# Attention logits of rows 0-127 and the indexer's dot products as three products of rounded parts, in a two-layer encoder on one core

## The chip, the core and the metric

The kernel runs on one NeuronCore of a Trainium2 chip as one launch. The metric is device time in microseconds (us). Five engines run in parallel, each through its own instructions in order: TensorE (PE, matmuls and transposes, its weight loads shown apart as PEld), VectorE (DVE), ScalarE (ACT), GpSimd (POOL) and SyncE (SP, which issues DMAs). They meet only at semaphores.

## The reference, cut to what matters

Two layers over 256 tokens of width 1024. All data is 32-bit float. In each layer:

```
h = rmsnorm(x);  z = h @ w_in          # split into qa ka va qi ki wi ga qb kb vb gb
# group A: 8 heads of 64, sparse attention
dots   = qi . ki / 8                   # 4 index heads of 64
iscore = sum_h relu(dots) * wi         # top 64 admissible keys of each query are kept
oa     = softmax(qa . ka / 8 over the kept keys) @ va
# group B: 4 heads of two maps, differential attention
ob = rmsnorm((softmax(q1 k1) - lambda softmax(q2 k2)) @ vb)
y  = concat(oa * silu(ga), ob * silu(gb)) @ w_out;  x = x + rmsnorm(y)
x  = x + rmsnorm((p @ w_ple_proj) * sigmoid(x @ w_ple_gate))
```

Rows 0 to 127 see keys 0 to 127 only; rows 128 to 255 see all 256. The change touches `dots` and the logits `qa . ka` and `q . k` of rows 0 to 127. The numbers computed stay the same but for rounding.

## The kernel before

**Tiling.** The tokens are two row blocks, b = 0 and b = 1, of 128 rows. Weights stream in as units of 256 rows by 512 columns (256 by 324 for the indexer's chunk). A large product is made of rounded parts: ScalarE copies a unit into a rounded 32-bit type (`w_hi`), VectorE subtracts that from the original (`w_lo`), and a matmul becomes three: high by high, low by high, high by low. One unit by one row block is a "piece": two groups of these three matmuls, 128 by 512. The activations are split in the same way (`act_hi`, `act_lo`).

**Order.** The function `layer_steps` writes one list of steps for a layer, and every engine walks the same list and does its part of each step. Pieces are the backbone; the attention steps are hung between them by the table `PLACE`, whose numbers count pieces from the first piece of the KB chunk (`mid`). Steps in the same slot are ordered by `rank`. `all_steps` adds the splitting of the next weight units (`HIGH` on ScalarE, `LOW` on VectorE).

**The steps the change touches.**
- `T chunk b`: PE transposes the four 128 by 128 tiles of a projected chunk into the one PSUM bank `tr` (L1332), and others empty it. For K, both blocks, and for Q, b = 1, ScalarE copies it rounded into `k_hi` or `q_hi` and VectorE then writes `k_lo` or `q_lo` (L934, L930). For Q, b = 0, ScalarE alone copies it whole into `qT`; for K, b = 0, ScalarE first makes a whole copy `kT` too.
- `TI b`: the same for the indexer's three tiles (L1321), copied whole by ScalarE into `idxT`, which lies in the memory of `pT`.
- `D`: the dot products (L1343), whole 32-bit matmuls, 64 rows deep. Odd and even heads use the two halves of the array's rows. ScalarE applies relu, VectorE sums the scores (L946, L948).
- `S n`: the logits (L1166). For b = 1 three products of `q_hi`, `q_lo`, `k_hi`, `k_lo`, 256 columns; for b = 0 one whole matmul `qT` by `kT`, 128 columns.
- `topk b r`: one round of the selection on VectorE (L961, L962); eight rounds for each block.
- `PT n`: PE transposes mixed probabilities into `tr` (L1375).

**One bank, one counter.** `TI`, `T` and `PT` all use `tr`. Each may start only when the previous user's bank is emptied: `wait_tr` waits on the counter `tr_out`, which the last reader of a step raises. In the trace a whole 32-bit matmul shows as two records, a rounded one as one.

Of the kernel before, what the change touches and what calls it, by code (L numbers as in the profile page):

```python
# [58 lines left out]
for _i, _u in enumerate(UNITS):  # L59
# [21 lines left out]
    S=[12, 15, 18, 34, 42, 43],  # L81
# [13 lines left out]
def layer_steps(L):  # L95
# [45 lines left out]
    else:  # L141
# [5 lines left out]
        mms("QB", one(1), {2: [("TI", 1)], 3: [("D",)]})  # L147

    mid = [[] for _ in range(7 * len(both))]
    placed = [(PLACE["lam"], ("lam",)), (PLACE["glu"], ("glu", 0))]  # L150
# [66 lines left out]
def build(nc, x, p, pre_norm_g, w_in, w_out, post_norm_g, lambda_q1, lambda_k1, lambda_q2, lambda_k2, subln_g,  # L217
# [6 lines left out]
    with ctx:  # L224
        def sb(name, shape, dt=fp32):
            return ctx.enter_context(nc.sbuf_tensor(name, shape, dt))
# [25 lines left out]
        k_lo = sb("k_lo", [P, 4, SEQ], f32r)  # L252
        q_hi = sb("q_hi", [P, 4, P], f32r)
        q_lo = sb("q_lo", [P, 4, P], f32r)

# [4 lines left out]
        idxT = pT[:, 0:2, :, :].rearrange("p a t q -> p (a t q)")[:, 0:3 * SEQ].rearrange("p (j t) -> p j t", j=3)  # L260
# [61 lines left out]
        qk_hi_done = sem("qk_hi_done")  # L322
        dots_done, relu_done, score_done = sem("dots_done"), sem("relu_done"), sem("score_done")
# [58 lines left out]
        QK_WHOLE = [("QB", 0), ("QA", 0)]  # L382
        QK_SPLIT = [s[1:] for s in tr_steps if s[0] == "T" and s[1:] not in QK_WHOLE]

# [209 lines left out]
        def _(act):  # L594
# [29 lines left out]
            for pos, (L, s) in enumerate(STEPS):  # L624
# [78 lines left out]
                elif kind == "TI":  # L703
                    b = s[1]
                    act.wait_ge(tr_done, tr_index(L, s))
                    copy(idxT[:, :, b * P:(b + 1) * P], tr[:, 0:3 * P].rearrange("p (j t) -> p j t", j=3))\
                        .then_inc(tr_out, 1)
                elif kind == "T":
                    chunk, b = s[1:]
                    act.wait_ge(tr_done, tr_index(L, s))  # L710
                    g, src = int(chunk[1] == "A"), tr[:, :].rearrange("p (j t) -> p j t", j=4)

                    if chunk[0] == "Q" and b == 0:
                        copy(qT[g][:, :, 0:P], src, HEAD ** -0.5).then_inc(tr_out, 1)
                    elif chunk[0] == "Q":
                        copy(q_hi[:, :, :], src, HEAD ** -0.5).then_inc(qk_hi_done, 1)
                    else:
                        if b == 0:
                            copy(kT[:, :, :], src)
                        copy(k_hi[:, :, b * P:(b + 1) * P], src).then_inc(qk_hi_done, 1)  # L720
# [76 lines left out]
        def _(dve):  # L797
# [31 lines left out]
            for pos, (L, s) in enumerate(STEPS):  # L829
# [94 lines left out]
                elif kind == "T" and s[1:] not in QK_WHOLE:  # L924
# [3 lines left out]
                    dve.wait_ge(qk_hi_done, L * 6 + QK_SPLIT.index(s[1:]) + 1)  # L928
                    if chunk[0] == "Q":
                        ins = nc.vector.scalar_tensor_tensor(q_lo[:, :, :], src, HEAD ** -0.5,  # L930
                                                             q_hi[:, :, :].bitcast(fp32), ALU.mult,
                                                             ALU.subtract)
# [3 lines left out]
                    ins.then_inc(tr_out, 1)  # L936
                elif kind == "D":
# [154 lines left out]
        def _(pe):  # L1092
# [60 lines left out]
            def logits(L, n, g, b, keys):  # L1153

                for j in range(N // keys):
                    for part in range(1 if b == 0 else 3):
                        for odd in range(2):
                            m = s_task(2 * n + odd)[2][j]
                            rows = slice(odd * HEAD, (odd + 1) * HEAD)
                            if b == 0:  # L1160
                                q, k = qT[g][rows, m // 2, 0:P], kT[rows, m // 2, :]
                            else:
                                q = (q_lo if part == 2 else q_hi)[rows, m // 2, :]
                                k = (k_lo if part == 1 else k_hi)[rows, m // 2, :]
                            end = part == (0 if b == 0 else 2)
# [20 lines left out]
            for pos, (L, s) in enumerate(STEPS):  # L1186
# [147 lines left out]
                elif kind == "D":  # L1334
# [3 lines left out]
                    for b in range(NB):  # L1338
                        keys = (b + 1) * P
                        for j in range(2):  # L1340
                            for odd in range(2):
                                rows = slice(odd * HEAD, (odd + 1) * HEAD)
                                ins = nc.tensor.matmul(dots_of(b, odd)[:, j * keys:(j + 1) * keys],  # L1343
                                                       idxT[rows, j, b * P:(b + 1) * P], idxT[rows, 2, 0:keys],
                                                       start=True, stop=True)
                                if j == 1:
                                    ins.then_inc(dots_done, 1)
# [82 lines left out]
```

## Time and profile before

| | us |
|---|---|
| median of 3 runs (lowest, highest) | 359.07 (358.68, 359.42) |
| the profiled execution's own time | 359.26 |
| its span, first to last instruction | 357.5 |
| PE busy | 350.0 (98%) |
| PE weight loads busy | 291.9 (82%) |
| VectorE busy | 264.5 (74%) |
| ScalarE busy | 228.6 (64%) |
| GpSimd busy | 67.2 (19%) |

The granted TensorE clock was 0.997 of full speed over the span. Busy time of PE overlaps its own pipeline (the next matmul starts before the last one's modelled end), so what a step of PE costs is read from the distance of two starts, not from the length of one record. The profiled execution is 1.76 us longer than its span and 0.19 us above the median of the runs.

### The profile page before, as it was taken

The page shows a single profiled execution, that of the slowest core. Times are in us where ns is not written, and L with a number is a line of the kernel's source. Part 1 is how long each engine was busy: PE and PEld are TensorE (multiplying, and loading weights), DVE is VectorE, ACT ScalarE, POOL GpSimd, SP SyncE. Part 2 cuts the span into 40 slices and gives each one's busy share as a digit, 9 for nine tenths or more (in the row PEclk, how much of TensorE's full clock was granted, in tenths as well). Part 3 has the DMA queues.
Part 4 walks back from the last instruction along what each step waited for, and adds up shares of the span by engine and source line. Part 5 has one row for each costly group of instructions (what it writes and reads, how often), then busy time and mean ns, then how long its engine had stood idle before and what let it go on. Part 6 is the DMA issues. An engine that isn't in the chain of part 4 may idle for free.

```text
span 357.5 us, 5709 instructions
## 1 busy us (share of the span) xinstructions
PE 350.0 (98%) x1927; PEld 291.9 (82%) x1927; DVE 264.5 (74%) x562; ACT 228.6 (64%) x459; POOL 67.2 (19%) x121
## 2 busy tenths in 40 slices
PE   8999999999999999999999999999999999999992
PEld 7887888888888888888888888788888888888882
DVE  3886979988946766786797487988895668678543
ACT  4897557777678945555757665778658686365221
POOL 1076261142200000013106433014220000000000
PEclk9999999999999999999999999999999999999998
DMA  7996488762754454647575927556355446550011
GB/s 287 381 336 216 130 193 200 257 177 68 224 169 131 129 195 149 210 158 154 179 231 158 353 82 207 147 129 178 107 168 155 151 141 213 175 169 11 0 50 69
DMA packets 31820, 61.12 MB, mean 171 GB/s; under 512 B 2376, under 2 KB 4432, under 8 KB 31792
## 3 DMA queue, kind: packets, MB, share of 16 engines
q1 hardware_dynamic: 30656, 57.48, 50.5%
q0 software_dynamic: 1120, 3.28, 4.8%
q8 instruction: 16, 0.26, 0.3%
q14 instruction: 12, 0.10, 0.1%
q10 hardware_dynamic: 16, 0.00, 0.0%
HBM read 59.71 MB, written 1.05 MB: 170 GB/s over the span
## 4 chain that ended last, share of the span: by engine, by line
PE 96%; issue 2%; DVE 1%; ACT 0%; POOLq 0%; DVEq 0%; POOL 0%
PE proj L1233 26%; PE proj L1235 25%; PE proj L1234 25%; PE sc L1314 3%; PE tr L1375 2%; PE sc L1166 2%; PE tr L1332 2%; PE pv L1396 2%; PE pv L1391 1%; PE proj L1177 1%; PE proj L1150 1%; PE proj L1166 1%; PE proj L1246 1%; PE proj L1139 1%; PE sc L1184 1%
## 5 line engine op out<-in xcount | busy, mean ns | idle before, releaser
L1233 PE MATMUL proj<-w_hi,act_hi 128*128 128x512 f32 (+1 forms) x392 | 157.4, 402 | 0.0
L1235 PE MATMUL proj<-w_hi,act_lo 128*128 128x512 f32 (+1 forms) x392 | 152.2, 388 | 0.0
L1234 PE MATMUL proj<-w_lo,act_hi 128*128 128x512 f32 (+1 forms) x392 | 151.6, 387 | 0.0
L835 DVE TENSOR_TENSOR w_lo<-raw,w_hi 128x1024 fp32r<-128x1024 f32 (+1 forms) x102 | 121.6, 1210 | 11.1 <-ACT w_hi L596 10.5
L596 ACT ACTIVATE w_hi<-raw 128x1024 fp32r<-128x1024 f32 (+2 forms) x103 | 102.5, 1022 | 2.4 <-PE proj L1235 1.8
L1235 PEld LDWEIGHTS proj<-w_hi,act_lo 128*128 128x128 f32 x392 | 73.5, 188 | 15.5
L1233 PEld LDWEIGHTS proj<-w_hi,act_hi 128*128 128x128 f32 x392 | 73.7, 188 | 14.6 <-issue 1.0
L1234 PEld LDWEIGHTS proj<-w_lo,act_hi 128*128 128x128 f32 x392 | 73.8, 188 | 12.8
L537 POOL TENSOR_TENSOR rstd<-var,minus_half 128x1 f32<-128x1 f32 x12 | 7.6, 640 | 191.6 <-DVE var L823 162.7
L732 ACT ACTIVATE probs<-probs,neg_max 128x128 f32<-128x128 f32 (+1 forms) x64 | 28.2, 444 | 6.0 <-DVE neg_max L986 6.0
L527 POOL TENSOR_TENSOR v_all<-work,rot_tab 128x128 f32<-128x128 f32 x16 | 10.6, 664 | 77.6 <-ACT work L596 77.5
L596 ACT ACTIVATE act_hi<-sc 128x512 fp32r<-128x512 f32 x20 | 11.3, 598 | 17.6 <-PE sc L1314 16.0
L596 ACT ACTIVATE pT<-tr 128x512 f32<-128x512 f32 (+1 forms) x20 | 11.4, 572 | 10.2 <-PE tr L1375 6.9
L915 DVE TENSOR_TENSOR act_lo<-sc,act_hi 128x512 fp32r<-128x512 f32 x16 | 10.4, 684 | 5.9 <-ACT act_hi L596 5.9
L934 DVE TENSOR_TENSOR k_lo<-tr,k_hi 128x512 fp32r<-128x512 f32 x8 | 5.5, 688 | 10.5 <-ACT k_hi L596 10.5
L732 ACT ACTIVATION_READ_ACCUMULATOR probs<-probs,neg_max 128x1 f32 x64 | 12.1, 189 | 0.0
L961 DVE MAX8 top<-score 128x8 f32<-128x128 f32 (+1 forms) x32 | 11.5, 358 | 0.6
L1375 PEld LDWEIGHTS tr<-ident,probs 128*128 128x128 f32 x72 | 8.8, 140 | 2.7 <-ACT pT L596 0.7
L962 DVE MATCH_REPLACE8 score<-top,score 128x128 f32<-128x128 f32 (+1 forms) x32 | 11.0, 343 | 0.0
L1375 PE MATMUL tr<-ident,probs 128*128 128x128 f32 x72 | 10.9, 273 | 0.0
L1051 DVE TENSOR_TENSOR work<-work,emb 128x512 f32<-128x512 f32 x7 | 4.8, 687 | 7.2 <-ACT work L768 7.2
L528 POOL TENSOR_TENSOR v_all<-work,rot_tab 128x64 f32<-128x64 f32 x16 | 10.1, 632 | 0.0
(209 smaller groups left out, 441.1 us busy)
## 6 DMA issues: line engine op xcount, KB each, us to landing
raw<-in_w_in_dram SPq DMA_DIRECT2D x59, 512.0 KB, 4.2
raw<-in_w_out_dram SPq DMA_DIRECT2D x16, 512.0 KB, 3.4
raw<-in_w_ple_gate_dram SPq DMA_DIRECT2D x16, 512.0 KB, 3.7
raw<-in_w_in_dram SPq DMA_DIRECT2D x7, 324.0 KB, 5.0
raw<-in_w_ple_proj_dram SPq DMA_DIRECT2D x4, 512.0 KB, 4.2
resid<-in_x_dram SPq DMA_DIRECT2D x2, 512.0 KB, 6.2
probs<-in_w_in_dram SPq DMA_DIRECT2D x2, 512.0 KB, 9.2
g_ple<-in_ple_norm_g_dram POOLq DMA_DIRECT2D x2, 512.0 KB, 7.3
```

The costliest lines, as they stand in the source:

```text
L527: nc.gpsimd.tensor_tensor(rot_a[:, 0:heads, :], view[:, :, 0:ROT], table(cos2, slice(0, ROT)), ALU.mult)
L596: return nc.scalar.activation(dst, src, ACT.Copy, scale=scale)
L732: last = nc.scalar.activation(probs[:, i % 4, j * keys:(j + 1) * keys], probs[:, i % 4, j * keys:(j + 1) * keys], ACT.Exp, bias=neg_max[:, ...
L835: nc.vector.tensor_tensor(w_lo[:, g % SLOTS, 0:nk * cols], landing(g, nk * cols), w_hi[:, g % SLOTS, 0:nk * cols].bitcast(fp32), ALU.subtr ...
L961: link(nc.vector.max(top8[:, :], score[b][:, :]))
L962: link(nc.vector.match_replace(score[b][:, :], top8[:, :], score[b][:, :], TAKEN))
L1166: ins = nc.tensor.matmul(s_bank(2 * n + odd)[:, j * keys:(j + 1) * keys], q, k, start=(part == 0), stop=end)
L1233: nc.tensor.matmul(ps, src_hi[:, b, k0 + k, :], hi, start=(first_u and k == 0), stop=False)
L1234: nc.tensor.matmul(ps, src_hi[:, b, k0 + k, :], lo, start=False, stop=False)
L1235: last = nc.tensor.matmul(ps, src_lo[:, b, k0 + k, :], hi, start=False, stop=last_k)
L1314: last = nc.tensor.transpose(sc[i % 2][:, j * P:(j + 1) * P], tile, ident[:, :])
L1375: last = nc.tensor.transpose(tr[:, j * P:(j + 1) * P], probs[:, si % 4, col:col + P], ident[:, :])
```

## The change

- The dot products of the indexer are made of rounded parts. ScalarE copies `tr` into `idx_hi`, VectorE writes `idx_lo` (both lie in `k_hi` and `k_lo`, which are free then), and VectorE, not ScalarE, now raises `tr_out`. Each of the 8 whole matmuls of a layer becomes three.
- The logits of rows 0 to 127 are made of rounded parts too. ScalarE writes `q0_hi`, VectorE `q0_lo` (in the memory of `p_hi` and `p_lo`) and raises `tr_out`. The whole copies `qT` and `kT` go. The 8 whole matmuls of each of the two groups become 24. Step `S` now waits for `k_lo`, not for `k_hi`.
- In layer 1 step `D` stands after the first piece of KB, not after the last of QB. In both layers step `S 3` (group A, rows 0 to 127) stands at slot 35, not 34.

```diff
-    S=[12, 15, 18, 34, 42, 43],
+    S=[12, 15, 18, 35, 42, 43],
...
-        mms("QB", one(1), {2: [("TI", 1)], 3: [("D",)]})
+        mms("QB", one(1), {2: [("TI", 1)]})
 
     mid = [[] for _ in range(7 * len(both))]
+    if L > 0:
+        mid[0].append(("D",))
...
+        idx_hi, idx_lo = k_hi[:, 0:3, :], k_lo[:, 0:3, :]
...
+        q0_hi, q0_lo = (tile[:, :, :, :].rearrange("p b k t -> p (b k) t") for tile in (p_hi, p_lo))
...
-        QK_WHOLE = [("QB", 0), ("QA", 0)]
-        QK_SPLIT = [s[1:] for s in tr_steps if s[0] == "T" and s[1:] not in QK_WHOLE]
+        QK_SPLIT = [s[1:] for s in tr_steps if s[0] == "T"]
...
                 elif kind == "TI":
                     b = s[1]
                     act.wait_ge(tr_done, tr_index(L, s))
-                    copy(idxT[:, :, b * P:(b + 1) * P], tr[:, 0:3 * P].rearrange("p (j t) -> p j t", j=3))\
-                        .then_inc(tr_out, 1)
+                    copy(idx_hi[:, :, b * P:(b + 1) * P], tr[:, 0:3 * P].rearrange("p (j t) -> p j t", j=3))\
+                        .then_inc(idx_hi_done, 1)
...
-                    if chunk[0] == "Q" and b == 0:
-                        copy(qT[g][:, :, 0:P], src, HEAD ** -0.5).then_inc(tr_out, 1)
-                    elif chunk[0] == "Q":
-                        copy(q_hi[:, :, :], src, HEAD ** -0.5).then_inc(qk_hi_done, 1)
+                    if chunk[0] == "Q":
+                        copy((q_hi if b else q0_hi)[:, :, :], src, HEAD ** -0.5).then_inc(qk_hi_done, 1)
                     else:
-                        if b == 0:
-                            copy(kT[:, :, :], src)
                         copy(k_hi[:, :, b * P:(b + 1) * P], src).then_inc(qk_hi_done, 1)
...
-                elif kind == "T" and s[1:] not in QK_WHOLE:
+                elif kind == "T":
...
-                    dve.wait_ge(qk_hi_done, L * 6 + QK_SPLIT.index(s[1:]) + 1)
+                    dve.wait_ge(qk_hi_done, L * 8 + QK_SPLIT.index(s[1:]) + 1)
                     if chunk[0] == "Q":
-                        ins = nc.vector.scalar_tensor_tensor(q_lo[:, :, :], src, HEAD ** -0.5,
-                                                             q_hi[:, :, :].bitcast(fp32), ALU.mult,
-                                                             ALU.subtract)
+                        hi, lo = (q_hi, q_lo) if b else (q0_hi, q0_lo)
+                        ins = nc.vector.scalar_tensor_tensor(lo[:, :, :], src, HEAD ** -0.5,
+                                                             hi[:, :, :].bitcast(fp32), ALU.mult, ALU.subtract)
...
+                elif kind == "TI":
+                    b = s[1]
+                    cols = slice(b * P, (b + 1) * P)
+                    dve.wait_ge(idx_hi_done, L * 2 + b + 1)
+                    nc.vector.tensor_tensor(idx_lo[:, :, cols], tr[:, 0:3 * P].rearrange("p (j t) -> p j t", j=3),
+                                            idx_hi[:, :, cols].bitcast(fp32), ALU.subtract).then_inc(tr_out, 1)
...
                 for j in range(N // keys):
-                    for part in range(1 if b == 0 else 3):
+                    for part in range(3):
                         for odd in range(2):
...
-                            if b == 0:
-                                q, k = qT[g][rows, m // 2, 0:P], kT[rows, m // 2, :]
-                            else:
-                                q = (q_lo if part == 2 else q_hi)[rows, m // 2, :]
-                                k = (k_lo if part == 1 else k_hi)[rows, m // 2, :]
-                            end = part == (0 if b == 0 else 2)
+                            hi, lo = (q_hi, q_lo) if b else (q0_hi, q0_lo)
+                            q = (lo if part == 2 else hi)[rows, m // 2, :]
+                            k = (k_lo if part == 1 else k_hi)[rows, m // 2, 0:keys]
+                            end = part == 2
...
                         for j in range(2):
-                            for odd in range(2):
+                            for part, odd in [(part, odd) for part in range(3) for odd in range(2)]:
...
+                                q, k = idx_lo if part == 2 else idx_hi, idx_lo if part == 1 else idx_hi
...
-                    if b == 0:
-                        pe.wait_ge(qk_hi_done, L * 6 + QK_SPLIT.index(keys_from) + 1)
-                    else:
-                        pe.wait_ge(tr_out, tr_index(L, ("T",) + keys_from))
+                    pe.wait_ge(tr_out, tr_index(L, ("T",) + keys_from))
```

How the instructions move, in the order in which each engine has them.

VectorE in layer 0, group A: the rounds of the selection for rows 128 to 255 (MAX, MATCH_REPLACE on `score`) around `T QA 0`. Before:

```order
L1010 SCALAR_TENSOR_TENSOR probs<-probs,mix_c 128x256
L961 MAX top<-score 128x8
L962 MATCH_REPLACE score<-top,score 128x256 [waits dve_chain]
L961 MAX top<-score 128x8 [waits dve_chain]
L962 MATCH_REPLACE score<-top,score 128x256 [waits dve_chain]
L961 MAX top<-score 128x8 [waits dve_chain]
L962 MATCH_REPLACE score<-top,score 128x256 [waits dve_chain]
L835 TENSOR_TENSOR w_lo<-raw,w_hi 128x1024 [waits hi_done,dve_chain]
```

After (`p_lo<-tr,p_hi` is `q0_lo`):

```order
L1016 SCALAR_TENSOR_TENSOR probs<-probs,mix_c 128x256
L967 MAX top<-score 128x8
L968 MATCH_REPLACE score<-top,score 128x256 [waits dve_chain]
L967 MAX top<-score 128x8 [waits dve_chain]
L968 MATCH_REPLACE score<-top,score 128x256 [waits dve_chain]
L931 SCALAR_TENSOR_TENSOR p_lo<-tr,p_hi 128x512 [waits qk_hi_done,dve_chain]
L967 MAX top<-score 128x8
L968 MATCH_REPLACE score<-top,score 128x256 [waits dve_chain]
L835 TENSOR_TENSOR w_lo<-raw,w_hi 128x1024 [waits hi_done,dve_chain]
```

A subtraction now stands behind the second of three rounds in a row; nothing stood there before. Layer 1 has the same rows at its own `T QA 0`.

PE in layer 1, the end of the QB chunk; `tr` and `pv` are the banks of the dot products. Before:

```order
L1235 MATMUL proj<-w_hi,act_lo 128x512
L1343 MATMUL tr<-pT 128x128 [waits at_lo,tr_out]
L1343 MATMUL pv<-pT 128x128
L1343 MATMUL tr<-pT 128x128
L1343 MATMUL pv<-pT 128x128
L1343 MATMUL sc<-pT 128x256 x4
L1233 MATMUL proj<-w_hi,act_hi 128x512 [waits at_lo,lo_done,idx_out]
L1234 MATMUL proj<-w_lo,act_hi 128x512
L1235 MATMUL proj<-w_hi,act_lo 128x512
L1233 MATMUL proj<-w_hi,act_hi 128x512
L1234 MATMUL proj<-w_lo,act_hi 128x512
L1235 MATMUL proj<-w_hi,act_lo 128x512
```

After (`k_hi` and `k_lo` hold `idx_hi` and `idx_lo`):

```order
L1237 MATMUL proj<-w_hi,act_hi 128x512 [waits at_lo,lo_done,idx_out]
L1238 MATMUL proj<-w_lo,act_hi 128x512
L1239 MATMUL proj<-w_hi,act_lo 128x512
L1237 MATMUL proj<-w_hi,act_hi 128x512
L1238 MATMUL proj<-w_lo,act_hi 128x512
L1239 MATMUL proj<-w_hi,act_lo 128x512
L1348 MATMUL tr<-k_hi 128x128 [waits at_lo,tr_out]
L1348 MATMUL pv<-k_hi 128x128
L1348 MATMUL tr<-k_lo,k_hi 128x128
L1348 MATMUL pv<-k_lo,k_hi 128x128
L1348 MATMUL tr<-k_hi,k_lo 128x128
L1348 MATMUL pv<-k_hi,k_lo 128x128
```

The dot products stand one piece, six matmuls, later, and are now single products of parts.

PE in layer 0, the logits of rows 0 to 127 of group B. Before:

```order
L1332 MATMUL tr<-ident,work 128x128 [waits rope_z,tr_out]
L1332 MATMUL tr<-ident,work 128x128 x3
L1166 MATMUL sc<-kT,qT_b 128x128 [waits relu_done,qk_hi_done]
L1166 MATMUL sc<-kT,qT_b 128x128 x7
L1233 MATMUL proj<-w_hi,act_hi 128x512 [waits at_lo,lo_done]
L1234 MATMUL proj<-w_lo,act_hi 128x512
L1235 MATMUL proj<-w_hi,act_lo 128x512
```

After (`p_hi` and `p_lo` hold `q0_hi` and `q0_lo`):

```order
L1336 MATMUL tr<-ident,work 128x128 [waits rope_z,tr_out]
L1336 MATMUL tr<-ident,work 128x128 x3
L1170 MATMUL sc<-k_hi,p_hi 128x128 [waits relu_done,tr_out]
L1170 MATMUL sc<-k_hi,p_hi 128x128
L1170 MATMUL sc<-k_lo,p_hi 128x128 x2
L1170 MATMUL sc<-k_hi,p_lo 128x128 x2
L1170 MATMUL sc<-k_hi,p_hi 128x128 x2
L1170 MATMUL sc<-k_lo,p_hi 128x128 x2
```

Eight matmuls became 24 (the pattern goes on for all four pairs of maps), and the wait is for `tr_out` in place of `qk_hi_done`.

## Rows read from the trace of the kernel before

**Rows 1.** Page: busy time, slices of VectorE, granted clock, chain by engine, w_lo.

```profile
PE 350.0 (98%) x1927; PEld 291.9 (82%) x1927; DVE 264.5 (74%) x562; ACT 228.6 (64%) x459; POOL 67.2 (19%) x121
...
DVE  3886979988946766786797487988895668678543
...
PEclk9999999999999999999999999999999999999998
...
PE 96%; issue 2%; DVE 1%; ACT 0%; POOLq 0%; DVEq 0%; POOL 0%
...
L835 DVE TENSOR_TENSOR w_lo<-raw,w_hi 128x1024 fp32r<-128x1024 f32 (+1 forms) x102 | 121.6, 1210 | 11.1 <-ACT w_hi L596 10.5
```

**Rows 2.** Timeline, PE, layer 0: start us, length us, engine, line, operation, count.

```profile
33.13 0.37 PE L1343 MATMUL tr<-pT 64*128 64x128 f32 x1
33.35 0.27 PE L1343 MATMUL tr<-pT 64*128 64x128 f32 x1
33.46 0.27 PE L1343 MATMUL tr<-pT 64*128 64x128 f32 x1
33.68 1.03 PE L1343 MATMUL sc<-pT 64*128 64x256 f32 x8
34.65 0.50 PE L1233 MATMUL proj<-w_hi,act_hi 128*128 128x512 f32 x1
```

**Rows 3.** Timeline, PE, layer 0: logits of rows 0-127, both head groups.

```profile
54.46 1.16 PE L1166 MATMUL sc<-kT,qT_b 64*128 64x128 f32 x16
...
93.13 1.16 PE L1166 MATMUL sc<-kT,qT_a 64*128 64x128 f32 x16
```

**Rows 4.** Timeline, PE, layer 0: logits of rows 128-255, second and last step.

```profile
60.10 0.28 PE L1166 MATMUL sc<-k_lo,q_hi 64*128 64x256 f32 x2
...
61.28 0.28 PE L1166 MATMUL proj<-k_hi,q_lo 64*128 64x256 f32 x2
```

**Rows 5.** Timeline, weight loads at the same place, the first two.

```profile
59.87 0.19 PEld L1166 LDWEIGHTS sc<-k_hi,q_hi 64*128 64x128 f32 x2 [0.35 <-issue]
59.98 0.19 PEld L1166 LDWEIGHTS sc<-k_lo,q_hi 64*128 64x128 f32 x2
```

**Rows 6.** Timeline, PE, layer 0: query transposes of group A, then probabilities.

```profile
77.99 0.60 PE L1332 MATMUL tr<-ident,work 128*128 128x128 f32 x4
...
79.36 0.39 PE L1234 MATMUL proj<-w_lo,act_hi 128*128 128x512 f32 x1
79.58 0.39 PE L1235 MATMUL proj<-w_hi,act_lo 128*128 128x512 f32 x1
79.81 0.60 PE L1375 MATMUL tr<-ident,probs 128*128 128x128 f32 x4
```

**Rows 7.** Timeline, ScalarE and VectorE, same stretch.

```profile
78.62 0.60 ACT L596 ACTIVATE qT_a<-tr 128x512 f32<-128x512 f32 x1 [0.46 <-PE tr L1332]
...
80.15 0.41 DVE L962 MATCH_REPLACE8 score<-top,score 128x256 f32<-128x256 f32 x1
80.59 0.43 DVE L961 MAX8 top<-score 128x8 f32<-128x256 f32 x1
```

**Rows 8.** Timeline, PE and VectorE, layer 1, the same place.

```profile
251.84 0.60 PE L1375 MATMUL tr<-ident,probs 128*128 128x128 f32 x4
...
252.54 0.43 DVE L961 MAX8 top<-score 128x8 f32<-128x256 f32 x1
```

**Rows 9.** Timeline, layer 1: the low part of group B, and who waits.

```profile
214.68 0.69 DVE L930 SCALAR_TENSOR_TENSOR q_lo<-tr,q_hi 128x512 fp32r<-128x512 f32 x1
...
215.42 0.42 PEld L1332 LDWEIGHTS tr<-ident,work 128*128 128x128 f32 x4 [0.33 <-DVE q_lo L930]
```

**Rows 10.** Timeline, layer 1: second index transposes copied, scores start.

```profile
203.78 0.49 ACT L596 ACTIVATE pT<-tr 128x384 f32<-128x384 f32 x1 [2.51 <-PE tr L1321]
...
206.51 0.43 DVE L946 TENSOR_SCALAR score<-probs,w_idx 128x128 f32<-128x128 f32 x1 [3.78 <-ACT probs L725]
```

**Rows 11.** Timeline, VectorE, layer 0: the low part of group A keys.

```profile
93.23 0.68 DVE L934 TENSOR_TENSOR k_lo<-tr,k_hi 128x512 fp32r<-128x512 f32 x1
```

More of the change, by code:

```diff
@@ L259, in build @@
         pT = sb("pT", [P, 3, 4, P])
-        idxT = pT[:, 0:2, :, :].rearrange("p a t q -> p (a t q)")[:, 0:3 * SEQ].rearrange("p (j t) -> p j t", j=3)
         score = [sb("score0", [P, P]), sb("score1", [P, SEQ])]
@@ L322, in build @@
         qk_hi_done = sem("qk_hi_done")
+        idx_hi_done = sem("idx_hi_done")
         dots_done, relu_done, score_done = sem("dots_done"), sem("relu_done"), sem("score_done")
@@ L710, in _ @@
                     act.wait_ge(tr_done, tr_index(L, s))
-                    g, src = int(chunk[1] == "A"), tr[:, :].rearrange("p (j t) -> p j t", j=4)
-                    if chunk[0] == "Q" and b == 0:
-                        copy(qT[g][:, :, 0:P], src, HEAD ** -0.5).then_inc(tr_out, 1)
-                    elif chunk[0] == "Q":
-                        copy(q_hi[:, :, :], src, HEAD ** -0.5).then_inc(qk_hi_done, 1)
-                    else:
-                        if b == 0:
-                            copy(kT[:, :, :], src)
+                    src = tr[:, :].rearrange("p (j t) -> p j t", j=4)
+                    if chunk[0] == "Q":
+                        copy((q_hi if b else q0_hi)[:, :, :], src, HEAD ** -0.5).then_inc(qk_hi_done, 1)
+                    else:
                         copy(k_hi[:, :, b * P:(b + 1) * P], src).then_inc(qk_hi_done, 1)
@@ L1340, in _ @@
                         for j in range(2):
-                            for odd in range(2):
+                            for part, odd in [(part, odd) for part in range(3) for odd in range(2)]:
                                 rows = slice(odd * HEAD, (odd + 1) * HEAD)
+                                q, k = idx_lo if part == 2 else idx_hi, idx_lo if part == 1 else idx_hi
                                 ins = nc.tensor.matmul(dots_of(b, odd)[:, j * keys:(j + 1) * keys],
-                                                       idxT[rows, j, b * P:(b + 1) * P], idxT[rows, 2, 0:keys],
-                                                       start=True, stop=True)
-                                if j == 1:
+                                                       q[rows, j, b * P:(b + 1) * P], k[rows, 2, 0:keys],
+                                                       start=(part == 0), stop=(part == 2))
+                                if j == 1 and part == 2:
                                     ins.then_inc(dots_done, 1)
```

## The prediction

> **What bounds the kernel.** First the page: PE is busy 98% of the span, at a granted clock of 0.9 or more in all slices but the last, and the chain that ended last runs over PE for 96% of its length [rows 1]. So what is added to PE's own work is added to the time, nearly one for one, and so is every stretch in which PE waits. VectorE is busy 74%, but not evenly: in many slices it stands at 8 or 9 tenths [rows 1]. That it has 93 us free over the span says nothing on a place where its queue is full. So I then read the timeline of PE at the steps that the change rewrites [rows 2 to 4], the weight loads there [rows 5], and the queues of VectorE and ScalarE at each step whose release of `tr` goes over to VectorE [rows 6 to 11].
>
> **What a step of PE costs.** Odd and even heads run as pairs on the two halves of the array; a pair is one step. Whole 32-bit at 128 columns: two records for each matmul, and the starts stand 0.11 us apart (33.35, 33.46) [rows 2]; 0.1115 with the next digit taken from whole blocks: 16 records of a block of logits take 1.16 us, of which 0.27 is the last one's own length and 0.10 the first load, and 0.78 over seven steps is 0.112 [rows 2, 3]. Whole at 256 columns: 8 records, 1.03 less a last length of 0.38, 0.65 over three steps, 0.216 [rows 2]. Rounded at 256 columns: from 60.10 to 61.28 lie ten steps, 0.118 each [rows 4]. Rounded at 128 columns is in no row; this is the disputed price p.
>
> Bounds of p. Below: rounded at 256 columns costs 0.118 and at 512 columns 0.22 to 0.23 (79.36 to 79.58 and to 79.81) [rows 4, 6]; the line through these, 0.11 per 256 columns, gives 0.06 at 128. Above: a narrow rounded matmul could be no better than a whole one of its size, two steps of 0.1115, 0.223 [rows 2]. Between them: at the head of a block, where nothing streams yet and PE's loader had been idle for 0.35 us, the second rounded weight load starts 0.11 us after the first (59.87, 59.98) [rows 5]. At that point only the load itself can hold it back, so a load takes about 0.11 us, and as each step needs one, 128 columns can't go faster than that however fast they stream. I take p = 0.1115, as for the whole ones, which load 128 columns too.
>
> The Trainium skill (TensorE: Matmul & The Clock Gate, "Back-to-back issue gap") gives about 81 ns for a matmul with its load at 128 columns in a long stream. By it the PE terms below would come to +0.1 us and not +1.9. No run here shows a step of 81 ns; the loads 0.11 us apart speak against it [rows 5].
>
> **Sum on PE.** Logits of rows 0 to 127: four blocks (two groups, two layers) of 8 steps become four of 12. Dot products of rows 0 to 127: two blocks of 4 become two of 6. Together 40 steps of 0.1115 = 4.46 become 60 p = 6.69: +2.23. Dot products of rows 128 to 255: 8 whole steps of 0.216 = 1.73 become 12 rounded of 0.118 = 1.42: -0.31. PE: +1.9. The gaps at the ends of such a block (first load, change to the halved array and back) are there with both kinds and don't change.
>
> **The wait I expect.** `T QA 0` leaves its transposes in `tr` at 78.4 (77.99 + four of 0.11) [rows 6]. Now ScalarE copies them at 78.62 and, by 79.22, frees `tr` [rows 7]; PE has one piece to do and begins `PT 2` in the same bank at 79.81 without a wait [rows 6]. After the change `tr` is free only when VectorE has written `q0_lo`. In its queue that stands behind the second of three rounds of the selection, and that round ends at 80.56, the third begins at 80.59 [rows 7]. Those rounds are paced by what lies before them (softmax of `S 2`, which PE and ScalarE feed), so they don't come earlier. `q0_lo` has the form of `q_lo`, 0.69 us [rows 9], so it ends at 81.28, and PE's load follows 0.05 later, as 215.42 follows 215.37 in [rows 9]: 81.33 in place of 79.81, 1.52, and 0.06 for the load that is no longer ahead. 1.58 us. Behind `PT 2` everything of PE is queued, so the loss is whole. Layer 1: 252.54 + 0.74 = 253.28 against 251.84 [rows 8], 1.44 + 0.06 = 1.50. Sum +3.1. If VectorE should come to it earlier, the term is 0; that is the lower end.
>
> **Other steps that now end on VectorE.** `T QB 0`: four pieces lie before the next use of `tr`, over 5 us; hidden. `TI 0`, `TI 1`: ScalarE's copy ends at 204.27 and the subtraction of 384 columns is shorter than 0.69 [rows 9, 10], so `idx_lo` is there by 204.9 to 205.0. `D` stood at 205.07; one piece later, after 205.07 + 6 x 0.23 = 206.45, it has 1.4 us of room. In layer 0 `D` has two pieces behind `TI 1`; hidden. The kT copies that go (two for each layer, 0.60 each by the same form of copy [rows 7]) are off the chain: 0.
>
> The move of `D` has a price on VectorE. The scores of layer 1 begin at 206.51, after VectorE was idle 3.78 us [rows 10]; they now begin one piece, 1.38, and two steps of 0.11 later, 1.6. One `w_lo`, 1.21 [rows 1], goes from behind them into that idle time before them. Net, VectorE reaches `q_lo` of `T QB 1` some 0.4 later. PE already waits there, though briefly: its load starts at 215.42, after 0.33 us of idling, released by `q_lo` [rows 9]. PE itself comes 0.06 later, so +0.35. In layer 0 the same place gets its dot products 0.2 later, and I take +0.1 for it by likeness. Together +0.5, between 0 and 0.9.
>
> `S 3` waits for `k_lo`: it ends at 93.23 + 0.68 = 93.91 [rows 11]. `S 3` stood at 93.13 [rows 3] and would have waited 0.8; at its new slot it comes at 94.5, later still by the 1.6 above, and even with VectorE 0.7 later it has room: 0. The slot takes one piece, 1.4 us, from the time before `PT 3` (slot 40), which needs the softmax of `S 3` and the bank; five pieces, 6.9 us, are left between them, and I take them as enough: 0.
>
> **Sum.** 1.9 + 3.1 + 0.5 = 5.5. On the profiled execution, 359.26, that is 364.8; it stands 0.19 above the median, so the forecast for the median is 359.07 + 5.5 = 364.6.
>
> **Rivals.**
> A, the above: 364.6, own range 363 to 366.5.
> B, narrow rounded matmuls cost as much as whole ones of their size, p = 0.223. 60 p = 13.4, so PE gets +8.9 - 0.3 = +8.6, and with both waits 359.07 + 8.6 + 3.6 = 371.2. For it: no row shows a rounded matmul below 256 columns. Against it: nothing from 512 to 256 columns hints at a fixed price, and the loads give a reason for 0.11 only.
> C, narrow steps stream at the columns' rate, p = 0.06: 3.6 - 4.5 - 0.3 = -1.2, with both waits and 0.2 less of the small ones, 359.07 + 2.2 = 361.2. For it: the line from 512 to 256 columns. Against it: [rows 5]. The Trainium skill (same page, "Weight-path perf modes") says that fast weight load is on for 128 weights of a type that is not FP32; were the rounded type such a one, C would be the case. The loads 0.11 us apart in this trace don't show it.
> D, the wait at `PT 2` doesn't form and p is 0.1115: 359.07 + 1.9 + 0.5 = 361.5. It would need VectorE to come to `q0_lo` by 79.1, 1.5 us before the trace has it there.
> E, not slower: the subtraction is taken before the rounds, so no wait forms at `PT 2`, and what is left hangs on p alone: 60 p - 4.46 - 0.31 + 0.5 is 0 at p = 0.071. Below this the kernel gains, at 0.06 by 0.7 us: 358.4. Place: `PT 2` in both layers. Against it both [rows 5] and [rows 7].
>
> **How the numbers follow.** A 0.57, B 0.21, C 0.13, D 0.06, E 0.03. The predicted time is A's. The range goes from 361.1, which takes in C and D, to 371.6 with B; about 0.15 is left out. What a measurement of this kernel can tell from no change is some 0.2%, 0.7 us: all but E lie beyond it. E is shared between faster, 0.02, and within, 0.01, with 0.01 more for what I have not seen; slower 0.96.
>
> **What would show it.** In the profile after: PE's pairs at 128 columns 0.11 us apart (0.06: C; 0.22, or two records for each matmul: B). An idle time of PE's loader of some 1.5 us before the transposes of probabilities of `PT 2`, put down to VectorE's `p_lo`, twice; none there would be D. One of 0.7 before the second QB transposes of layer 1, put down to `q_lo`. The dot products of rows 128 to 255 at 0.118 a step. PE busy up by about 2 us, less than the span. I am wrong if the span grows by less than 3 us or by more than 8.

## The result and the profile after

| | before | after |
|---|---|---|
| median, us (4 runs each, side by side) | 359.25 | 363.73 |
| lowest, highest | 358.68, 359.53 | 363.49, 364.12 |
| span of the profiled execution | 357.5 | 361.8 |

The ratio is 1.0128, with a 95% interval from 1.0114 to 1.0142: 4.5 us slower (4.1 to 5.1).

The page of the kernel after: busy times, and the chain that ended last by engine.

```profile
PE 351.7 (97%) x1975; PEld 293.8 (81%) x1975; DVE 268.7 (74%) x570; ACT 226.8 (63%) x455; POOL 67.5 (19%) x121
...
PE 92%; DVE 3%; issue 2%; ACT 2%; POOLq 0%; DVEq 0%; POOL 0%
```

Against [rows 1], PE is busy only 1.7 us more, though the span grew by 4.3: less than half is matmul work. The share of VectorE in the chain went from 1% to 3%, that of ScalarE from 0% to 2%. So at some places PE is now released by VectorE, behind work that ScalarE feeds.

The timeline of PE at the logits of rows 0 to 127 of group B, layer 0, after (12 steps; the first three and the last, and what follows):

```profile
54.10 0.33 PE L1170 MATMUL sc<-k_hi,p_hi 64*128 64x128 f32 x2
54.26 0.28 PE L1170 MATMUL sc<-k_lo,p_hi 64*128 64x128 f32 x2
54.37 0.28 PE L1170 MATMUL sc<-k_hi,p_lo 64*128 64x128 f32 x2
...
55.38 0.28 PE L1170 MATMUL sc<-k_hi,p_lo 64*128 64x128 f32 x2
55.59 0.51 PE L1237 MATMUL proj<-w_hi,act_hi 128*128 128x512 f32 x1
```

From the second start, 54.26, to the twelfth, 55.38, lie ten steps: 0.112 us each, the price of a whole step of that width [rows 2, 3]. The first step takes 0.16 (54.10 to 54.26), where the first whole one took 0.22 (33.13 to 33.35 in [rows 2]). So the block should be longer by four steps, 0.45, less 0.05. The starts say the same: it and the way to the next piece took 1.49 us (54.10 to 55.59), where the block before took 1.09 (54.46 [rows 3] to 55.55).

The timeline of PE's weight loads at the next place, `PT 2` of layer 0, after (in brackets the idle time before, and who ended it), and then that of VectorE in the same stretch:

```profile
79.37 0.19 PEld L1239 LDWEIGHTS proj<-w_hi,act_lo 128*128 128x128 f32 x1
81.36 0.42 PEld L1377 LDWEIGHTS tr<-ident,probs 128*128 128x128 f32 x4 [1.81 <-DVE p_lo L931]
81.75 0.19 PEld L1237 LDWEIGHTS proj<-w_hi,act_hi 128*128 128x128 f32 x1
```

```profile
78.66 0.42 DVE L967 MAX8 top<-score 128x8 f32<-128x256 f32 x1
...
79.64 0.43 DVE L967 MAX8 top<-score 128x8 f32<-128x256 f32 x1
...
80.18 0.41 DVE L968 MATCH_REPLACE8 score<-top,score 128x256 f32<-128x256 f32 x1
80.62 0.69 DVE L931 SCALAR_TENSOR_TENSOR p_lo<-tr,p_hi 128x512 fp32r<-128x512 f32 x1
81.23 0.42 DVE L967 MAX8 top<-score 128x8 f32<-128x256 f32 x1
```

This answers to [rows 6, 7]. The probabilities' transposes began at 79.81, right behind the piece before them [rows 6]; now their weight load comes at 81.36, after 1.81 us in which the loader idled, released by `p_lo`, VectorE's subtraction for `q0_lo`. That begins at 80.62, behind two rounds of the selection (78.66 and 79.64, so 0.98 us a round), where the third stood (80.59 in [rows 7]). The chain that ended last, in order of time, runs here from ScalarE's exponentials over the mixing of the maps and these two rounds to the subtraction. Two of its pieces, the exponentials and the last one ahead of PE:

```profile
75.77 1.48 ACT probs L732 x6
...
80.62 0.70 DVE p_lo L931
```

The subtraction and the load that it releases in layer 1, from the same timelines:

```profile
255.02 0.69 DVE L931 SCALAR_TENSOR_TENSOR p_lo<-tr,p_hi 128x512 fp32r<-128x512 f32 x1
255.76 0.42 PEld L1377 LDWEIGHTS tr<-ident,probs 128*128 128x128 f32 x4 [1.72 <-DVE p_lo L931]
```

### The profile page after: what moved, and what is told of

Read it like the earlier page. It is cut to its first block, busy times and chain, and to the rows that moved or that the text cites. A ratio compares the mean times of both kernels' runs of the same rounds, so it can differ in the third digit from the quotient of the medians.

```text
span 361.8 us, 5811 instructions
## 1 busy us (share of the span) xinstructions
PE 351.7 (97%) x1975; PEld 293.8 (81%) x1975; DVE 268.7 (74%) x570; ACT 226.8 (63%) x455; POOL 67.5 (19%) x121
## 4 chain that ended last, share of the span: by engine, by line
PE 92%; DVE 3%; issue 2%; ACT 2%; POOLq 0%; DVEq 0%; POOL 0%
PE proj L1237 25%; PE proj L1239 24%; PE proj L1238 24%; PE sc L1170 3%; PE sc L1318 2%; PE tr L1377 2%; PE tr L1336 2%; PE pv L1398 2%; PE proj L1156 1%; PE proj L1181 1%; ACT probs L732 1%; PE pv L1393 1%; PE proj L1170 1%; PE proj L1145 1%; PE sc L1188 1%
## 5 line engine op out<-in xcount | busy, mean ns | idle before, releaser
L1237 PE MATMUL proj<-w_hi,act_hi 128*128 128x512 f32 (+1 forms) x392 | 157.5, 402 | 0.0
L1237 PEld LDWEIGHTS proj<-w_hi,act_hi 128*128 128x128 f32 x392 | 73.7, 188 | 14.0 <-issue 0.3
L600 ACT ACTIVATE pT<-tr 128x512 f32<-128x512 f32 x16 | 9.5, 595 | 9.7 <-PE tr L1377 9.7
L600 ACT ACTIVATE k_hi<-tr 128x512 fp32r<-128x512 f32 (+1 forms) x12 | 6.7, 559 | 11.4 <-PE tr L1336 7.8
L536 POOL TENSOR_TENSOR work<-v_all 128x128 f32<-128x128 f32 x16 | 10.3, 643 | 1.3
```

Source lines behind the costliest of these rows:

```text
L600: return nc.scalar.activation(dst, src, ACT.Copy, scale=scale)
L1237: nc.tensor.matmul(ps, src_hi[:, b, k0 + k, :], hi, start=(first_u and k == 0), stop=False)
```

## Where the time went, place by place

The start-up of an execution differs: the first whole piece of PE's steady work begins at 21.35 us in the profile before, at 20.84 in the one after, and between 20.99 and 23.99 in those of the experiments. So I took the start of the first matmul of each group of three, of which a piece has two (L1233 before, L1237 after, the same line of code, 400 of them), in each trace, and read where its distance from the same start before changes. Everything from 21 us on is in this table, in us; the columns are the kernels, the last row is the sum of all changes of the distance to the end of the span.

| place | after | wait_only | logits_only | dots_only | rounds0 | rounds1 | pt2_later | s34_pt27 | half_load |
|---|---|---|---|---|---|---|---|---|---|
| dot products and `q_lo`, layer 0 | +0.16 | 0 | 0 | +0.14 | +0.15 | +0.04 | +0.04 | +0.14 | +0.15 |
| logits group B, layer 0 | +0.36 | 0 | +0.36 | 0 | +0.36 | +0.36 | +0.35 | +0.36 | -0.26 |
| `PT 2`, layer 0 | +1.59 | +1.55 | +1.58 | 0 | +0.24 | +0.57 | +0.21 | +0.21 | +1.58 |
| logits group A, layer 0 | +0.41 | 0 | +0.41 | 0 | +0.41 | +0.41 | +0.41 | +1.22 | -0.23 |
| dot products and `q_lo`, layer 1 | +0.04 | 0 | 0 | +0.03 | +0.03 | +0.03 | +0.04 | +0.03 | +0.04 |
| logits group B, layer 1 | +0.39 | 0 | +0.39 | 0 | +0.39 | +0.39 | +0.39 | +0.39 | -0.23 |
| `PT 2`, layer 1 | +1.52 | +1.53 | +1.48 | 0 | +0.26 | +0.53 | +0.14 | +0.14 | +1.48 |
| logits group A, layer 1 | +0.41 | 0 | +0.41 | 0 | +0.41 | +0.41 | +0.41 | +1.17 | -0.23 |
| all from 21 us on | +4.88 | +2.89 | +4.57 | +0.02 | +2.20 | +2.70 | +2.00 | +3.61 | +2.30 |

Changes below 0.03 are written as 0. Two traces are not in the table, d_old and rounds1_pt27; their sums stand with their runs. A column's places add up to its last row within 0.2: some hundredths lie between the places, and that is how fine this comparison of two executions is. The profile after thus holds 3.1 us of waits at `PT 2`, 1.6 of logits, 0.2 at the dot products and `q_lo`, and it started 0.5 sooner: 4.9 - 0.5 = 4.4, against 4.3 in the spans.

## The experiments

Medians are of the runs of that kernel, with those of the kernel before on the same chip beside them.

| kernel | median | before beside it | ratio (95% interval) |
|---|---|---|---|
| wait_only | 362.28 | 359.23 | 1.0087 (1.0062 to 1.0113) |
| logits_only | 364.92 | 359.23 | 1.0149 (1.0122 to 1.0176) |
| dots_only | 359.51 | 359.23 | 1.0002 (0.9983 to 1.0020) |
| pt2_later | 361.03 | 359.23 | 1.0047 (1.0032 to 1.0061) |
| rounds0 | 362.64 | 359.38 | 1.0083 (1.0058 to 1.0108) |
| half_load | 361.71 | 359.38 | 1.0063 (1.0040 to 1.0086) |
| s34_pt27 | 362.97 | 359.38 | 1.0102 (1.0075 to 1.0130) |
| d_old | 364.52 | 359.38 | 1.0145 (1.0120 to 1.0170) |
| rounds1 | 362.25 | 359.04 | 1.0089 (1.0076 to 1.0102) |
| rounds1_pt27 | 361.10 | 359.04 | 1.0071 (1.0051 to 1.0092) |

An interval is up to 2 us wide, and the medians hold the start-up, which moves by more than the differences in question. So differences of some tenths are read from the table of places and not from the medians.

**The wait alone** (on the kernel before).

```diff
...
-                    if chunk[0] == "Q" and b == 0:
+                    if chunk == "QA" and b == 0:
+                        copy(qT[g][:, :, 0:P], src, HEAD ** -0.5).then_inc(qa0_done, 1)
+                    elif chunk[0] == "Q" and b == 0:
...
+                elif kind == "T" and s[1:] == ("QA", 0):
+                    dve.wait_ge(qa0_done, L + 1)
+                    nc.vector.scalar_tensor_tensor(p_lo[:, :, :, :].rearrange("p b k t -> p (b k) t"),
+                                                   tr[:, :].rearrange("p (j t) -> p j t", j=4), HEAD ** -0.5,
+                                                   qT[1][:, :, 0:P], ALU.mult, ALU.subtract).then_inc(tr_out, 1)
```

> The kernel before, with one thing added: at T QA 0, in both layers, VectorE subtracts from tr (its result, written to the free low part of p, is used by nobody), and VectorE in place of ScalarE raises tr_out. No matmul changes. Theory A (the late release of tr makes PE wait at PT 2, and the wait is paid in full): 3.1 us slower than before, 362.3; loader idle of 1.8 before PT 2 in each layer, put down to that VectorE instruction. Rival (the wait is made up by other engines' slack, and the time of the change is matmul work): within 0.5 us of before.

3.05 us slower by the medians, 2.9 by the trace from 21 us on. The timeline of the weight loads and of VectorE in its trace, at `PT 2` of layer 0:

```profile
80.89 0.19 PEld L1243 LDWEIGHTS proj<-w_hi,act_lo 128*128 128x128 f32 x1
...
82.12 0.69 DVE L929 SCALAR_TENSOR_TENSOR p_lo<-tr,qT_a 128x512 fp32r<-128x512 f32 x1
82.86 0.20 PEld L1383 LDWEIGHTS tr<-ident,probs 128*128 128x128 f32 x2 [1.79 <-DVE p_lo L929]
```

Not one matmul is changed here, and the wait is the same, 1.79 us of an idle loader. Theory A holds: one late release of `tr` in each layer costs PE 1.5 to 1.6 us, and at most 0.2 of the 3.1 us is given back later.

**The logits alone** (on the kernel after).

```diff
-        mms("QB", one(1), {2: [("TI", 1)]})
+        mms("QB", one(1), {2: [("TI", 1)], 3: [("D",)]})
...
-    if L > 0:
-        mid[0].append(("D",))
...
-                    copy(idx_hi[:, :, b * P:(b + 1) * P], tr[:, 0:3 * P].rearrange("p (j t) -> p j t", j=3))\
-                        .then_inc(idx_hi_done, 1)
+                    copy(idxT[:, :, b * P:(b + 1) * P], tr[:, 0:3 * P].rearrange("p (j t) -> p j t", j=3))\
+                        .then_inc(tr_out, 1)
...
-                            for part, odd in [(part, odd) for part in range(3) for odd in range(2)]:
+                            for odd in range(2):
```

> The changed kernel with the index heads' part undone: dot products whole again, D at its old place in layer 1. The logits of rows 0 to 127 stay in three products. Theory A: 1.55 us of matmuls (four blocks, 0.39 each as measured after) and 3.1 us of waits: 4.6 slower than before, 363.8 or 0.3 less than after. If the index part costs more than its matmuls show, 362.5 or less.

By the places 4.6 us from 21 us on, as expected. The median says 5.7, 1.1 more than expected; the six runs spread from 363.55 to 365.93, and the interval, 4.4 to 6.3, takes in the 4.6. The places say 0.3 less than after, which is what the index part adds there.

**The dot products alone** (on the kernel before; `D` of layer 1 one piece later, as in the change).

```diff
-        mms("QB", one(1), {2: [("TI", 1)], 3: [("D",)]})
+        mms("QB", one(1), {2: [("TI", 1)]})
...
+    if L > 0:
+        mid[0].append(("D",))
...
-                    copy(idxT[:, :, b * P:(b + 1) * P], tr[:, 0:3 * P].rearrange("p (j t) -> p j t", j=3))\
-                        .then_inc(tr_out, 1)
+                    copy(idx_hi[:, :, b * P:(b + 1) * P], tr[:, 0:3 * P].rearrange("p (j t) -> p j t", j=3))\
+                        .then_inc(idx_hi_done, 1)
...
+                elif kind == "TI":
...
-                            for odd in range(2):
+                            for part, odd in [(part, odd) for part in range(3) for odd in range(2)]:
```

> The kernel before with the index heads' part of the change alone: dot products from rounded parts in three products, D of layer 1 one piece later. Theory A: matmuls +0.07 in each layer, +0.1 for q_lo in layer 0, nothing in layer 1: 0.3 us slower than before, 359.5, hardly to be told from it. Rival (VectorE's two more subtractions in each layer push the chain of selection and so PE): 1 us or more slower.

Not to be told from the kernel before: 1.0002, and 0.7 us slower at the upper end of the interval. The places show 0.14 in layer 0 and 0.03 in layer 1, and the rest of its sum is below what such a comparison of two executions resolves. The rival, that two more subtractions for each layer push VectorE's chain and cost 1 us or more, is out.

**`PT 2` one slot later** (on the kernel after).

```diff
-    PT=[19, 23, 26, 40, 41, 45, 46, 50, 51],
+    PT=[19, 23, 27, 40, 41, 45, 46, 50, 51],
```

> The changed kernel with PT 2 one slot later (27 in place of 26), one more piece between the transposes of T QA 0 and the next use of tr. Theory A: q0_lo ends at 81.3, PE comes at 81.2, so the wait goes from 1.6 to 0.1 to 0.2 in each layer: 2.9 us faster than after, 360.8. Rival: PV 2 at 28 then waits for ScalarE's copy of pT and gives part of it back, 361.5 to 362.

361.03 where 360.8 was expected. The places give 2.9 us back, as expected: the wait fell from 1.6 and 1.5 to 0.2 and 0.14. No new wait shows at `PV 2`, so the rival is out.

**No round, and one round, before the subtraction** (on the kernel after).

```diff
-    topk=[[0, 0, 2, 6, 6, 7, 10, 11], [12, 24, 24, 25, 26, 26, 27, 31]],
+    topk=[[0, 0, 2, 6, 6, 7, 10, 11], [12, 25, 25, 25, 26, 26, 27, 31]],   # rounds0
+    topk=[[0, 0, 2, 6, 6, 7, 10, 11], [12, 24, 25, 25, 26, 26, 27, 31]],   # rounds1
```

> The changed kernel with the two rounds of selection of rows 128 to 255 that stood at slot 24 moved to slot 25, behind T QA 0, so that no round stands between the mixing of the maps and the subtraction. Theory A (the place in VectorE's queue makes the wait): ScalarE's copy ends at 79.2, q0_lo at 79.9, PE comes at 79.8; wait 0.15 to 0.2 in each layer in place of 1.6: 2.8 us faster than after, 360.9. Rival (the subtraction itself and its hand-over make most of it): 1 us faster at most.

> The changed kernel with one of the two rounds of selection of slot 24 moved behind T QA 0, so that one round stands before the subtraction. A round takes 0.98 us of VectorE. With two rounds the wait at PT 2 cost PE 1.60 and 1.51 us, with none 0.25. Theory A (the wait is the queue ahead of the subtraction): 1.6 - 0.98 = 0.6 in each layer, 2.0 us faster than after. Rival (any round ahead costs the same, for instance because the selection starts late anyway): 1.6 again.

The timeline of the weight loads of `PT 2`, layer 0, in the kernel with no round ahead:

```profile
81.08 0.20 PEld L1377 LDWEIGHTS tr<-ident,probs 128*128 128x128 f32 x2 [0.45 <-DVE p_lo L931]
```

and in the one with one round ahead:

```profile
81.12 0.20 PEld L1377 LDWEIGHTS tr<-ident,probs 128*128 128x128 f32 x2 [0.80 <-DVE p_lo L931]
```

The cost is 1.59, 0.57, 0.24 in layer 0 with two, one and no round ahead, and 1.52, 0.53, 0.26 in layer 1. From two to one it falls by 1.0, the length of a round (0.98, above). From one to none it can fall by 0.3 only, since then ScalarE's copy ends last; VectorE waited for it, as its timeline in rounds0 shows:

```profile
80.34 0.69 DVE L931 SCALAR_TENSOR_TENSOR p_lo<-tr,p_hi 128x512 fp32r<-128x512 f32 x1 [0.52 <-ACT p_hi L600]
```

So the late release is what stood ahead of the subtraction in its queue. The median of rounds0, 362.64, is above the 360.9 expected. Its places say 2.2 us from 21 us on, 2.7 less than after, where 2.8 was expected, and its profiled execution, 362.06, is those 2.2 and a start 0.6 later than before. The six runs spread from 361.68 to 363.75, so nothing rests on that median but that the kernel is slower than before. The median of rounds1, 362.25, is 3.2 above the kernel before beside it, where 2.5 was expected; its places say 2.7, 2.2 less than after where 2.0 was expected, and its profiled execution started 0.4 later than that of before.

**Both, as the best order for the new arithmetic.**

```diff
-    PT=[19, 23, 26, 40, 41, 45, 46, 50, 51],
+    PT=[19, 23, 27, 40, 41, 45, 46, 50, 51],
...
-    topk=[[0, 0, 2, 6, 6, 7, 10, 11], [12, 24, 24, 25, 26, 26, 27, 31]],
+    topk=[[0, 0, 2, 6, 6, 7, 10, 11], [12, 24, 25, 25, 26, 26, 27, 31]],
```

> The changed kernel with one round moved behind T QA 0 and PT 2 at slot 27: the best order for the changed arithmetic that the runs so far point to. Theory A: no wait is left at PT 2 in either layer; what stays over the kernel before is matmul work, 1.55 for the logits and 0.15 for the dot products, and 0.1 at q_lo: 1.8 us slower than before, 361.1. If it is as fast as before, the matmul work is not what the rest costs.

361.1 expected, 361.10 measured. That the two agree to the last digit is chance: the kernel before ran at 359.04 beside it, so it is 2.1 slower by the medians and 1.0071 by the ratio, with 1.8 expected. In the timeline of its weight loads the one of `PT 2` has no idle time ahead of it:

```profile
81.68 0.14 PEld L1377 LDWEIGHTS tr<-ident,probs 128*128 128x128 f32 x1
```

Its places come to 1.5 us from 21 us on: logits 0.36, 0.40, 0.39 and 0.40, nothing at `PT 2`. With no wait left at `PT 2` the changed kernel is still behind the one before, by its matmuls. No version with the split logits is as fast as the kernel before.

**Half the weights** (on the kernel after; logits of rows 0 to 127 for 64 of the 128 query rows, the others left out).

```diff
-                            q = (lo if part == 2 else hi)[rows, m // 2, :]
+                            q = (lo if part == 2 else hi)[rows, m // 2, 0:P if b else P // 2]
...
-                            ins = nc.tensor.matmul(s_bank(2 * n + odd)[:, j * keys:(j + 1) * keys], q, k,
+                            ins = nc.tensor.matmul(s_bank(2 * n + odd)[0:P if b else P // 2, j * keys:(j + 1) * keys], q, k,
```

> The changed kernel with the logits of rows 0 to 127 computed for 64 of the 128 query rows only (the other 64 rows are left out): each of the 96 pairs of matmuls still streams 128 columns, but loads 64 columns of weights. Theory A (at 128 columns the load sets the distance of the steps): the step falls from 0.108 to 0.055 to 0.07, 48 steps, 1.8 to 2.5 us faster than after. Rival (128 columns of the rounded type stream at half rate): the step stays at 0.107, same time as after.

Its timeline of PE at the logits of group B, layer 0, second, third and last step:

```profile
54.87 0.23 PE L1170 MATMUL sc<-k_lo,p_hi 64*64 64x128 f32 x2
54.93 0.22 PE L1170 MATMUL sc<-k_hi,p_lo 64*64 64x128 f32 x2
...
55.46 0.22 PE L1170 MATMUL sc<-k_hi,p_lo 64*64 64x128 f32 x2
```

From 54.93 to 55.46 are nine steps, 0.059 each, with the same 128 columns streamed as in the kernel after, where a step took 0.112. Halving the load halved the step. The run uses half the width of the array too, but at full width the stream isn't what holds the step: 256 columns took 0.118 [rows 4], so 128 would take 0.06. And at the head of a block, where the loader comes from an idle time, two loads of 64 weights stand 0.05 apart, where two of 128 stood 0.11 apart [rows 5]:

```profile
54.76 0.13 PEld L1170 LDWEIGHTS sc<-k_hi,p_hi 64*64 64x64 f32 x2 [0.17 <-issue]
54.81 0.14 PEld L1170 LDWEIGHTS sc<-k_lo,p_hi 64*64 64x64 f32 x2
```

So at 128 columns it is the load of 128 weights that sets the step, and the rounded type streams at least as fast as 0.06 us for 128 columns. The places give 2.6 us back where 1.8 to 2.5 was expected, 48 steps of 0.053. The kernel also shows what rival C would have measured: 2.3 us over the kernel before, by the medians and by the places, where the prediction had 2.2.

**`S 3` back at slot 34** (on the kernel with `PT` at 27).

```diff
-    S=[12, 15, 18, 35, 42, 43],
+    S=[12, 15, 18, 34, 42, 43],
```

> The changed kernel with PT 2 at 27 (wait gone) and S 3 back at its old slot 34. Theory: S 3 needs k_lo, which ends at about 94.6 while PE is there at 93.5: a wait of 0.8 to 1.3 in each layer, 1.6 to 2.6 slower than the run with PT 2 at 27 alone (361.0). Rival: k_lo is there in time and the move to 35 was for nothing: 361.0.

Its timeline of VectorE's `k_lo` and the logits' first load, layer 0:

```profile
93.59 0.69 DVE L934 TENSOR_TENSOR k_lo<-tr,k_hi 128x512 fp32r<-128x512 f32 x1
94.33 0.19 PEld L1170 LDWEIGHTS sc<-k_hi,p_hi 64*128 64x128 f32 x2 [1.17 <-DVE k_lo L934]
```

A wait of 1.17 us of the loader, 0.81 and 0.76 in the places (1.22 less 0.41, 1.17 less 0.41). Together 1.6 slower than pt2_later by the places and 1.8 by the medians, each against the kernel before beside it, with 1.6 to 2.6 expected. The move to 35 was needed, and did what it had to.

**`D` of layer 1 at its old place** (on the kernel after).

```diff
-        mms("QB", one(1), {2: [("TI", 1)]})
+        mms("QB", one(1), {2: [("TI", 1)], 3: [("D",)]})
...
-    if L > 0:
-        mid[0].append(("D",))
```

> The changed kernel with D of layer 1 at its old place, behind the last piece of QB. idx_lo of TI 1 ended at 206.91 in the trace after and PE would come at 207.10, so PE waits 0 to 0.1: same time as after within 0.2 us. If it is over 0.5 slower, the hand-over at tr is longer than I read it; if over 0.3 faster, the move had a price on VectorE that I don't see.

Its timeline of the weight loads at `D` of layer 1 (`k_hi` and `k_lo` here are the memory of `idx_hi` and `idx_lo`):

```profile
208.10 0.18 PEld L1346 LDWEIGHTS tr<-k_hi 64*128 64x128 f32 x1 [0.36 <-DVE k_lo L939]
```

The loader idled 0.36 us there, released by `k_lo`, hardly more than the 0.35 that its loader idles anyway when the array changes to halves [rows 5]. The places come to 4.6 from 21 us on, 0.2 less than after, 0.1 of it at `q_lo` in layer 0, where nothing differs between the two kernels. The median is 364.52, 5.1 above the kernel before beside it (interval 4.3 to 6.1), where the changed kernel was 4.5 above: 0.7 slower, past the 0.5 that the expectation named as a sign of a longer hand-over. The places don't bear that out: no wait is there, and its profiled execution began its steady work 1.1 us later than that of after (21.98 and 20.84). So the move of `D` neither gains nor costs anything that these runs can tell.

## Why the prediction was right, and where it was off

The forecast was 5.5 us slower, 364.6; the medians say 4.5 and the places 4.9. Of the 1.0 too much, 0.2 lies in the logits and 0.4 in `q_lo` (below). The rest is about as large as the 0.5 by which the profiled execution after happened to start sooner; no run shows it to be due to the change, and no step of the prediction has it.

- **PE bounds the kernel, so what PE gets is paid.** Right: 4.9 us from 21 us on are found again in PE's starts at the places of the table.
- **The price p, taken as 0.1115.** Right: 0.112 measured. The step was argued from two loads 0.11 apart [rows 5]; half_load shows that the load sets the step, which until then was only argued. Of the Trainium skill's two rules that I weighed (TensorE: Matmul & The Clock Gate, "Back-to-back issue gap" and "Weight-path perf modes"), the 81 ns and the fast weight load would both give less. The traces agree with neither for this type: a step took 0.112 us and two loads of 128 weights stand 0.11 apart.
- **PE's sum, +1.9.** Somewhat large, and the smaller of two terms that were off: 0.36 to 0.41 for a block of logits where four steps of 0.1115 make 0.45, together 1.57 in place of 1.78. I took the ends of a block to be the same with both kinds, but the first rounded step is 0.05 shorter (0.16 and 0.21 in the logits). The dot products came at 0.07 for each layer, from 32.27 to 34.17 in the profile after where 32.82 to 34.65 was before, as in the sum.
- **The wait at `PT 2`, 1.58 and 1.50.** Right to a few hundredths: 1.59 and 1.52. The 0.06 for the load stood in the forecast without a row; it is there: from the first transpose to the next piece PE took 0.42 (81.36 to 81.78), and 0.36 before (79.81 to 80.17). The wait was read from one queue, in time (where VectorE is) and in order (what stands ahead). The runs with the wait alone and with two, one and no round show the cause.
- **`q_lo`, +0.5 in all.** The term that was mis-sized. Layer 0 got 0.12 (0.1 forecast, by likeness), but in pt2_later, rounds1, rounds1_pt27 and d_old, which are the same kernel up to there, it got nothing; so that it was met is partly luck. Layer 1 got -0.03 where +0.35 was forecast, and the sign that was named for it, an idle loader of 0.7 us, didn't come; it idled 0.30, as before (0.33 in [rows 9]):

```profile
217.51 0.42 PEld L1336 LDWEIGHTS tr<-ident,work 128*128 128x128 f32 x4 [0.30 <-DVE q_lo L931]
```

  The scores did begin about 1.5 us later, and a `w_lo` went from behind them to before them, as forecast. But the scores of rows 0 to 127 took 0.36 less, so VectorE came to `q_lo` when it had before (1.5 less 1.2 less 0.36). The timeline of layer 1 after at that place, VectorE and then GpSimd:

```profile
210.09 0.29 DVE L952 TENSOR_SCALAR score<-probs,w_idx 128x128 f32<-128x128 f32 x1 [1.56 <-ACT probs L725]
210.41 1.13 DVE L954 SCALAR_TENSOR_TENSOR score<-probs,w_idx,score 128x128 f32<-128x128 f32 x3
...
209.47 0.46 POOL L536 TENSOR_TENSOR work<-v_all 128x128 f32<-128x128 f32 x1
```

and the same in wait_only, which has `D` where the kernel before has it:

```profile
209.59 0.43 DVE L954 TENSOR_SCALAR score<-probs,w_idx 128x128 f32<-128x128 f32 x1 [4.25 <-ACT probs L728]
210.06 0.96 DVE L956 SCALAR_TENSOR_TENSOR score<-probs,w_idx,score 128x128 f32<-128x128 f32 x2
...
209.62 0.32 POOL L531 TENSOR_TENSOR v_all<-work,rot_tab 128x64 f32<-128x64 f32 x1
210.02 0.46 POOL L533 TENSOR_TENSOR work<-v_all 128x128 f32<-128x128 f32 x1
```

  With GpSimd's rotation of the next chunk beside the first two of the four instructions, the four took 1.81 to 1.82 us (before, wait_only, logits_only); with GpSimd done they took 1.45 in all eight traces that have `D` moved. In d_old, with `D` back at its old place, they took 1.66:

```profile
209.58 0.32 POOL L532 TENSOR_TENSOR v_all<-work,rot_tab 128x64 f32<-128x64 f32 x1
209.98 0.46 POOL L534 TENSOR_TENSOR work<-v_all 128x128 f32<-128x128 f32 x1
...
209.71 0.29 DVE L950 TENSOR_SCALAR score<-probs,w_idx 128x128 f32<-128x128 f32 x1 [1.82 <-ACT probs L723]
210.03 0.95 DVE L952 SCALAR_TENSOR_TENSOR score<-probs,w_idx,score 128x128 f32<-128x128 f32 x2
```

  There the first took 0.29 though the end of a GpSimd instruction lay beside it, and only the second was long. So the 0.36 has two parts: with the dot products split they took 0.16 less (logits_only against d_old), and with `D` moved another 0.21 (d_old against after). That either works by way of GpSimd is argued from the times that lie side by side, and wasn't tried apart.
- **Hidden steps.** Right: no wait appeared at `T QB 0`, at `D`, at `S 3` or at `PT 3`. That the kT copies went shows as no gain at any place.
- **The rivals.** B would need steps of 0.22, C of 0.06, D no wait at `PT 2`; none is there. E would need steps below 0.071 and no wait, and the best order shows the sum without any wait: still 1.5 us by the trace, 0.7% by the runs.

## What to carry to other kernels

In this kernel three products of rounded parts were cheaper than one whole matmul at 256 columns (0.35 against 0.43 us for a pair) and dearer at 128 (0.34 against 0.22), where the weight load and not the stream sets the step. When the release of a shared bank goes over to another engine, look at what stands ahead in that engine's queue at that moment, not at its busy share: VectorE had a quarter of its time free and still cost 3 us. In an engine at 98%, order is worth as much as arithmetic: one number in the table of places gave back 2.9 of the 4.9 us.

## What the runs showed of the hardware

- At 128 columns a step of rounded matmuls with 128 weights took 0.112 us; with 64 weights it took 0.059.
- The first step of a block in halves of the array took 0.16 us with rounded operands and 0.21 to 0.22 with whole ones.
- A VectorE instruction on 128 columns took 0.43 us in three traces with GpSimd at work beside it and 0.29 in the eight with GpSimd done; in d_old it took 0.29 with the end of a GpSimd instruction beside it.
- Start-up differed by up to 3.2 us between the profiled executions (first full piece at 20.84 to 23.99 us). For changes of 1% it pays to compare traces from a point behind it.
